# An up-projection with its weights held still, and four stage ends in another order

## What is computed

```
D_MODEL, D_FF, SEQ, CONV_WIDTH = 2048, 5632, 256, 3
def conv_ffn(h, w_up, conv_w, conv_b, w_down):
    up = h @ w_up                                   # 256 x 11264
    up_p = pad(up, two rows of zeros before the first token)
    c = conv_b + sum(conv_w[j] * up_p[:, j:j + S] for j in range(3))
    gate, val = split(c, 2, axis=-1)
    return (silu(gate) * val) @ w_down
...
x = x + conv_ffn(rmsnorm(x, ffn_norm_g), w_up, conv_w, conv_b, w_down)
...
h = layer_norm(ALPHA * h + fox(h)); h = layer_norm(ALPHA * h + retention(h))
```

## Time and profile before

| | us |
|---|---|
| median of 3 runs | 2361.91 (2361.75 to 2361.94) |
| the profiled execution | 2361.47 |
| its span in the trace | 2359.3 |
| busy in the span: PE, DVE, ACT | 2339.5, 1493.4, 1156.0 |
| first multiplication of weights starts | 8.76 |
| FFN: its first matmul, and fox's first | 366.58, 1111.18 |
| retention's first matmul | 1602.46 |

### The profile page before, as it was taken

One profiled execution on the slowest core, in us unless ns is written; L12 is line 12 of the kernel. 1 busy time (PEld: TensorE's weight loads), 2 busy tenths in 40 slices (PEclk: granted clock), 3 DMA queues, 4 the chain that ended last, 5 costly groups with the idle time before them and its releaser, 6 DMA issues.

```text
span 2359.3 us, 30665 instructions
## 1 busy us (share of the span) xinstructions
PE 2339.5 (99%) x10778; PEld 1930.6 (82%) x10778; DVE 1493.4 (63%) x1977; ACT 1156.0 (49%) x1531; POOL 46.6 (2%) x60
## 2 busy tenths in 40 slices
PE   9999999999999999999999999999999999999998
PEld 8788888888888888887888888887888888887886
DVE  5567576666666666668556666677556456456557
ACT  6544545555554555555454444455444434444443
POOL 0000000000000000000000000000000000000000
PEclk9999999999999999999999999999999999999999
DMA  9556546656656666665689559955755655665644
GB/s 319 157 171 204 165 149 185 188 183 190 185 180 189 189 195 186 184 190 175 214 174 185 178 175 172 176 187 171 224 169 180 191 173 178 196 188 158 197 154 143
DMA packets 220385, 434.63 MB, mean 184 GB/s; under 512 B 13360, under 2 KB 13520, under 8 KB 219520
## 3 DMA queue, kind: packets, MB, share of 16 engines
q1 hardware_dynamic: 218384, 422.76, 61.7%
q0 software_dynamic: 1616, 10.44, 1.2%
q10 hardware_dynamic: 288, 0.10, 0.0%
HBM read 431.05 MB, written 2.11 MB: 184 GB/s over the span
## 4 chain that ended last, share of the span: by engine, by line
PE 96%; DVE 3%; ACT 0%; issue 0%; DMA 0%; DVEq 0%; POOL 0%; ACTq 0%
PE acc L513 90%; PE mix L513 3%; PE mix L801 1%; DVE w_lo L1388 1%; DVE res L1398 1%; PE mix L569 0%; PE mix L645 0%; PE mix L878 0%; PE mix L900 0%; PE mix L661 0%; DVE res L1960 0%; PE mix L676 0%; DMA ident_sb<-const_ident 0%; DVE arena L1696 0%; DVE res L1969 0%
## 5 line engine op out<-in xcount | busy, mean ns | idle before, releaser
L1388 DVE TENSOR_TENSOR w_lo<-raw,w_hi 128x1024 fp32r<-128x1024 f32 x790 | 963.0, 1222 | 573.7 <-ACT w_hi L980 569.8
L980 ACT ACTIVATE w_hi<-raw 128x1024 fp32r<-128x1024 f32 x791 | 836.3, 1059 | 743.3 <-PE acc L513 710.9
L513 PE MATMUL acc<-w_hi,x_hi 128*128 128x512 f32 x2352 | 938.1, 399 | 2.5 <-DVE w_lo L1388 1.7
L513 PE MATMUL acc<-w_hi,x_lo 128*128 128x512 f32 x2352 | 917.5, 390 | 0.0
L513 PE MATMUL acc<-w_lo,x_hi 128*128 128x512 f32 x2352 | 915.4, 389 | 0.0
L513 PEld LDWEIGHTS acc<-w_hi,x_lo 128*128 128x128 f32 x2352 | 441.4, 188 | 94.6
L513 PEld LDWEIGHTS acc<-w_hi,x_hi 128*128 128x128 f32 x2352 | 441.8, 188 | 93.7 <-issue 6.5
L513 PEld LDWEIGHTS acc<-w_lo,x_hi 128*128 128x128 f32 x2352 | 442.3, 188 | 88.7 <-issue 1.4
L513 PE MATMUL acc<-w_hi,y_hi 128*128 128x512 f32 x800 | 316.5, 396 | 3.4 <-DVE y_lo L1531 2.1
L513 PE MATMUL acc<-w_hi,y_lo 128*128 128x512 f32 x800 | 311.7, 390 | 0.0
L513 PE MATMUL acc<-w_lo,y_hi 128*128 128x512 f32 x800 | 311.4, 389 | 0.0
(11 more groups left out here) (192 smaller groups left out, 1055.5 us busy)
## 6 DMA issues: line engine op xcount, KB each, us to landing
raw<-in_ret_w_in SPq DMA_DIRECT2D x192, 512.0 KB, 3.9
raw<-in_w_up SPq DMA_DIRECT2D x176, 512.0 KB, 4.2
raw<-in_fox_w_in SPq DMA_DIRECT2D x128, 512.0 KB, 5.3
raw<-in_w_down SPq DMA_DIRECT2D x88, 512.0 KB, 4.5
raw<-in_w_in SPq DMA_DIRECT2D x80, 512.0 KB, 3.7
raw<-in_ret_w_out SPq DMA_DIRECT2D x64, 512.0 KB, 4.1
raw<-in_w_out SPq DMA_DIRECT2D x32, 512.0 KB, 3.8
raw<-in_fox_w_out SPq DMA_DIRECT2D x32, 512.0 KB, 4.4
```

Of the source, the lines that this page charges most:

```text
L513: return nc.tensor.matmul(o, l, r, start=start, stop=stop)
L980: return nc.scalar.activation(o, i_, f, **kw)
L1388: V.tensor_tensor(lo, raw[:, g.base % RAW, :], hi, ALU.subtract).then_inc(lo_done, 1)
```

## The change

In the FFN's up-projection the weights become the stationary operand. `columns_block` holds a 128x128 tile of `w_hi` and moves `x_hi` and `x_lo` side by side past it (`x_both`, 512 columns, into the two halves of a PSUM bank), then a tile of `w_lo` with `x_hi` alone (256 columns). Channels are on partitions at once: a block of 512 channels fills four banks, gate and value blocks take turns on `acc` and `mix`, and the down-projection of the pair before goes through the banks that this pair's gate has left. ACT copies the second halves out, DVE adds the first halves and multiplies by the norm's factor, now a row over tokens (`rbc`, made by one more matmul of `ones` with `diag`). Taps, gate and product work on tiles of up to four channel groups at a time. The drains to `z` and the transpositions of line 801 are gone.

Four stage ends: at the start, the first chunk goes through in halves, the identity moves to POOL's queue and 15 warm matmuls stand in place of 18; at the end of the FFN, the last pair's product and `y` go in halves a phase earlier, and DVE adds before it splits; between fox and retention, sums are taken along with the additions and squares by ACT, the first two feature tiles are transposed apart, and the first chunk is split earlier; in the last layer norm, token tile 0 is centred into `z` and ahead of `row_add_out(1, 0)`.

Of the diff: `columns_block` is PE's; `columns_out`, `scale_rows` and `value_part` are DVE's (the last runs in the eight slots of a down-projection); `first_halves` is ACT's at the start, and DVE has its like; `ln_squares_of` is ACT's between fox and retention, after each slot's split.

```diff
-WARM_START, WARM_NORM = 18, (14, 6)
+WARM_START, WARM_NORM = 15, (12, 4)
...
+            def columns_block(g, free, banks, step, build=False):
+                for c in range(CH):
+                    if build:
+                        pe.wait_ge(xt_lo, 8 + c + 1)
+                    pe.wait_ge(lo_done, g.at(c + 1))
+                    slot = (g.base + c) % SPLIT
+                    for half in (FFN_B % 2, 1 - FFN_B % 2):
+                        if c == 0:
+                            for blk in free[half != FFN_B % 2]:
+                                block_out(pe, blk)
+                        for k in range(KC):
+                            kt = c * KC + k
+                            for f in (2 * half, 2 * half + 1):
+                                at = slice(k * COL + f * P, k * COL + (f + 1) * P)
+                                o = banks[:, f, :].rearrange("p (a s) -> p a s", a=2)
+                                if kt > 0:
+                                    mm(o[:, 0, :], w_lo[:, slot, at], x_hi[:, kt, :], False, False)
+                                done = mm(o, w_hi[:, slot, at], x_both[:, :, kt, :], kt == 0, kt == KT - 1)
+                                if kt == 0:
+                                    mm(o[:, 0, :], w_lo[:, slot, at], x_hi[:, kt, :], False, False)
...
+            def columns_out(blk, pair, a, banks):
+                v.wait_ge(u_copied[a], pair.at(1))
+                u = up[a][:, :, 2:S + 2]
+                V.tensor_tensor(u, banks[:, :, 0:S], u, ALU.add).then_inc(drained[blk.base % 2], 1)
+                block_out(v, blk)
+            def scale_rows(pair, a):
+                u = up[a][:, :, 2:S + 2]
+                V.tensor_tensor(u, u, rbc.rearrange("p (o s) -> p o s", o=1).to_broadcast([P, 4, S]), ALU.mult)\
+                    .then_inc(u_up[a], 1)
+            def value_part(pair, blk, odd, y0):
+                def step(s):
+                    if s == 0:
+                        columns_out(blk, pair, 1, ffn_banks(odd)[1])
+                        scale_rows(pair, 1)
+                    elif s in (2, 4):
+                        taps_of(pair, 1, s // 2 - 1)
+                    elif s == 5:
+                        product(pair)
+                    elif s == 7:
+                        low(pair, y0)
...
+            def first_halves():
+                act.wait_ge(x_full[0], 16)
+                for k in range(KC):
+                    a_(x_hi[:, k, :], xT[:, k, :], ACT.Copy, scale=gains[:, G_ATT + k:G_ATT + k + 1])\
+                        .then_inc(xt_hi if k else first_hi, 1)
+                    act.wait_ge(raw_full[0] if k else first_raw, 16)
+                    c = slice(k * COL, (k + 1) * COL)
+                    a_(w_hi[:, 0, c], raw[:, 0, c], ACT.Copy).then_inc(hi_done if k else first_hi, 1)
...
+            def ln_squares_of(nb):
...
+                    done = a_(z[:, (4, 5, 0, 1)[nb], t, :], res[:, t, nb * COL:(nb + 1) * COL], ACT.Square, scale=D ** -0.5,
+                              bias=ln_stat[:, 0, t:t + 1], accum_out=ln_squares[:, t, nb:nb + 1])
...
             v.wait_ge(ln_full, 64)
-            row_add_out(1, 0)
             v.wait_ge(row_mean, 2)
-            v.wait_ge(row_var, 1)
             row_centre(0, 0, D // 2)
             row_centre(0, D // 2, D // 2)
+            row_add_out(1, 0)
             row_scale(0)
```

More of the change, by code:

```diff
@@ new lines, in down, with scales @@
+            def down(g, blk, y0, banks, kt, last=-2):
+                per = kt // KC
+                for s in range(NOUT * per):
+                    nb, c = s // per, s % per
+                    if c == 0:
+                        block_out(pe, blk.plus(nb - 2 if nb >= 2 else last))
+                    chunk(g.plus(s), (blk.base + nb) % 2, y_hi, y_lo, y0 + c * KC, c == 0, c == per - 1, banks=banks)
+            def scales(s):
+                if s == 4:
+                    block_out(pe, Count(FFN_B))
+                    pe.wait_ge(d_full, 2)
+                    mm(acc[0][0][:, 0:S], ones[:], diag, True, True).then_inc(rbc_mm, 1)
@@ L1006, in xt_out @@
             def xt_out(phase, j):
+                if phase == 3 and j == 0:
+                    for k in range(2):
+                        if k == 0:
+                            act.wait_ge(ln_first_t, 1)
+                        else:
+                            act.wait_ge(ln_first_aff, 1)
+                        a_(x_hi[:, k, :], M[3 * k][:, 0:S], ACT.Identity, scale=gains[:, G_LG + k:G_LG + k + 1],
+                           bias=gains[:, G_LB + k:G_LB + k + 1]).then_inc(xt_hi if k else ln_first_hi, 1)
+                    return
                 if phase == 3:
@@ L1722, in _ @@
[L1722 to L1733 removed]
+            for a in range(2):
+                done = V.memset(up[a][:, :, 0:2], 0.0)
@@ new lines, in scales, with first_pair @@
+            def scales(s):
+                if s == 0:
+                    columns_out(Count(FFN_B), Count(0), 0, acc_banks)
+                elif s == 2:
+                    v.wait_ge(got, 4)
+                    for t in range(TOK):
+                        done = V.tensor_scalar(diag[:, t * P:(t + 1) * P], ident[:], rs[:, t:t + 1], None, ALU.mult)
+                    done.then_inc(d_full, 1)
+            def first_pair(s):
+                pair = Count(0)
+                if s == 0:
+                    columns_out(Count(FFN_B + 1), pair, 1, mix_banks)
+                    v.wait_ge(rbc_sb, 2)
+                    scale_rows(pair, 0)
+                elif s == 1:
+                    scale_rows(pair, 1)
+                elif s in (2, 3):
+                    taps_of(pair, 0, s - 2)
+                elif s in (4, 5):
+                    taps_of(pair, 1, s - 4)
+                    if s == 5:
+                        gated(pair)
+                elif s == 6:
+                    product(pair)
+                elif s == 7:
+                    low(pair, 0)
```

521 lines of the change are left out of this document (330 added, 191 removed).

## The result

| | before | after |
|---|---|---|
| median | 2361.83 (4 runs, 2361.75 to 2361.94) | 2348.26 (4 runs, 2347.95 to 2348.96) |
| the profiled execution | 2361.47 | 2347.95 |
| its span | 2359.3 | 2345.7 |
| busy: PE, DVE, ACT | 2339.5, 1493.4, 1156.0 | 2329.1, 1528.2, 1134.3 |

What follows compares the result with a forecast made beforehand. PE's own list of matmuls was taken to bound the kernel. The terms -20.8 + 7.0 + 0.5 - 1.6 - 1.1 - 0.9 - 0.8 = -17.7 us gave 2344.2 us, range 2338 to 2357.

Steps and rivals of the forecast that it cites:

- The bound: Whole kernel: PE, busy 99% of the span, sets the end by its instructions' number and cost, not by waits.
- Part 1: FFN: 176 transpositions, 44 groups at 0.472 us each, leave PE's path, -20.8 us.
- Part 2: FFN up-projection: six matmuls of 512 columns become four of 512 and four of 256, +7.0 us.
- (a): Rival, FFN up-projection: a 512 after a 256 keeps the slow pace of 0.235 us, 2355.9 us; chance 0.2.
- What has to keep up: FFN down-projection: DVE falls behind by one or two us with 5.8 us to spare; costed at 0.
- Rival (c): DVE's lag in the down-projection reaches PE; each us beyond costs 10 us over the pairs; chance 0.07.
- Part 3: FFN's end: PE's waits for DVE's late additions go as work moves ahead, -1.6 us, between -1.6 and 0.
- Part 4: Start: first chunk in halves lets PE start about 1.6 us sooner; -1.1 us, between -0.5 and -1.5.
- Part 5: Fox to retention: POOL starts 0.35 us sooner, third chunk gains 0.6; -0.9 us, between 0 and -2.5.
- Part 6: Tail: centring in DVE's idle time lets its last addition meet PE, -0.8 us, between -0.8 and 0.
- Rival (d): Up-projection: weight loads no longer hide behind short matmuls, 99 us more, 2443; chance 0.05, shared with split-operand cost.

## Why the prediction was right or wrong

**The bound.** Right. PE's list sets the time; four more additions a pair on DVE changed nothing.

**Part 1, transpositions, -20.8.** Right as far as the sum shows; it was not undone by itself. The FFN's 732.69 us are, within 0.2, the forecast's terms with only the couple's price put right: -20.8 + 0.5 - 1.6 + 7.0 + 3.2 = -11.7, and 11.93 were measured.

**Part 2, +7.0, the term that was mis-sized: it measured +10.2.** 1408 couples at 347.3 instead of 345.0 ns. Two steps failed. The 118.3 of the narrow block was taken as the price of a 256 with no check in another place. In long streams it is 120.0, whichever operand changes, and 226.7 + 120.0 is the steady couple: 1.7 ns a couple, 2.4 us. That is an agreement of sums and not a cause, since the single distances are 231 to 233 and 112 to 117; and why the narrow block, with 112 to 123 ns from start to start all through, comes to 118.3 stays open. And the head of each block, the matmuls behind it and the one block at 353.3 add 0.6 ns a couple on average, 0.9 us. "With 0.345 us a pair there is time to refill" was wrong as a reason: the 512s stay slow, 231 to 233, and the 256s are quicker in return. The Trainium skill's N / 2.4 + 2.5 ns ("TensorE: Matmul & The Clock Gate", section "Back-to-back issue gap"), which the page gives for the gap of a single matmul and by which the time would have been lower still, doesn't hold in any stream here: 13.3 ns stand in place of its 2.5 at 256, 384 and 512 columns. (In the forecast's working by that formula the two added instructions are 5.0 ns a step and not 5.2; the 1.8 us are right.) What the same operands can do (353.3 with another head) was no term of the forecast but a rival's, (a), and it was nearer than its 0.2 said: another order of eight couples gives it in 18 blocks of 22. Nothing in the forecast's reasons told 346.7 from 353.3; that the kernel falls on the cheaper pattern, and so comes out near the likeliest time and not near the range's upper end, was luck.

**What has to keep up, 0.** Right, and for the reason given: 5.8 us to spare were worked out, 5.0 and 0.94 of idle time measured. Rival (c) didn't happen. Its price, "each us beyond costs 10 us over the pairs", left out the clock: with nine pairs and 3.9 us beyond it was 14.

**Part 3, the FFN's end, -1.6.** Right, and a little low: the last 180 matmuls of the FFN, up to fox's first transposition, took 44.57 us before with four groups of transpositions (1.89) among them, and take 40.83 now, 1.85 less for the end itself. PE has no gap left there, and DVE waits for PE instead (0.30 us ahead of each addition). It was not undone by itself.

**Part 4, the start, -1.1: measured -0.75.** PE starts at 7.26, 1.50 sooner (1.6 forecast). But "PE gets to it at 11.5 to 11.6" was the arrival of the kernel before; from 7.1 it is 9.9, and the second chunk's `w_lo` ends at 10.42. So PE waits for it where 1.1 us were said to be spare:

```profile
9.19 1.23 DVE L1534 TENSOR_TENSOR w_lo<-raw,w_hi 128x1024 fp32r<-128x1024 f32 x1
...
10.56 0.47 PE L530 MATMUL acc<-w_hi,x_both 128*128 128x512 f32 x1 [0.28 <-DVE w_lo L1534]
```

The third chunk starts at 13.37 instead of 14.32, -0.95, and 0.2 of that is lost before the FFN; by what was not looked into. The clock did stay up (1.00 from 7.3 on).

**Part 5, fox to retention, -0.9: measured -0.17.** POOL started 3.27 us behind the first warm matmul where it was 3.37 before, 0.1 for the 0.35 that were counted: the last squares end at 1583.93 and DVE's two small instructions and the hand-overs take 0.55. The rest is a step that the forecast didn't have, the clock: the first warm group is over at 1584.0, the transpositions start 2.31 us later at half clock and take 1.97 us. Part 4 had a sentence about the clock, part 5 had none. The forecast spoke of the third chunk: it starts 15.00 us behind the first warm matmul before, 14.82 after and 14.12 with 21 warm matmuls. With the clock kept up the -0.9 is there, -0.88 with 21 warm matmuls and -0.87 with 12 in the one execution where it stayed up.

**Part 6, the tail, -0.8.** Right: -0.78. DVE's last addition now waits 0.78 us for PE, as said, where it was late before:

```profile
2335.55 0.69 DVE L2217 TENSOR_TENSOR res<-acc,res 128x512 f32<-128x512 f32 x1 [0.78 <-PE acc L530]
```

**Rival (d)** can be left: loads of 187 to 192 ns stood under matmuls 120.0 ns apart in the streams, as in the narrow block.

**The range** (2338 to 2357) held it. Its upper end was real, (a), which another order at the blocks' heads gives. Its lower end, a 256 at half of a 512 with the 512 as before, came in no run: where the 256s were that quick, the 512s paid for it.

## What to carry to other kernels

Take the price of a short matmul from a long stream of its own kind, not from one short stretch of another kernel, and when lengths mix expect the long ones to be slow for five instructions; try the order at a block's head, since it can pick a steady pattern 2% apart, and read every block, since what ran ahead has a say in it. Where an edit shortens what PE does while it waits, look at the granted clock behind the wait as well as at the wait, and in more than one execution. When a start is moved ahead, move every arrival behind it by as much before asking what is spare.

## What the runs showed of the hardware

Couples of 512 and 256 columns have two steady patterns, 346.7 and 353.3 ns, kept to the end of a stream (88 couples and more) or block. In streams the order of the first eight couples picked one; pieces, banks, weights' places and a lead of 24 long matmuls made no difference. In the kernels what ran ahead counts as well: the same head was followed by 353.3 in the changed kernel's third block, and by either in the run with eight additions. A single 256 among 512s costs 113 ns and 28 ns more in the five matmuls behind it. What queue or buffer does this stays open: no run looked inside. The fixed part of a matmul with a new weight load was 13.3 ns at 256, 384 and 512 columns, and 128 columns took 111.7 ns, which is near to 120 and far from 66.7. An idle time of 3.8 us was followed by a granted clock of 0.50 to 0.53 nine times out of nine; one of 2.0 to 2.3 us, behind a group of 12 or 14 warm matmuls, seven times out of nine. And at a loop's first turn PE stands still for nothing that a row shows, by up to 1.1 us, and goes on 1.7 to 1.9 us behind the end of a transfer on the instruction queue.
